# Attention values with their low halves stacked beside them in the mixer of a two-block transformer kernel

## The chip, the cores and the metric

The kernel runs as one program on one core of a Trainium2 chip. The metric is the device time of one execution in microseconds. Three runs of the kernel before gave a median of 1433.6 us, the lowest 1432.47, the highest 1434.11.

## The reference

The program computes two blocks on an input of 512 tokens by 1024 features, in float32. The first block has a mixer (a state-space branch and an attention branch side by side), a merge of the two and a feed-forward part; the second has two more mixers. The change sits in the attention branch of the first mixer, which has 8 heads of 64 features:

```python
def one_block(args):
    blk, q_blk = args
    q_pos = blk * Q_BLOCK + jnp.arange(Q_BLOCK)
    z = jnp.einsum('bqhd,bkhd->bhqk', q_blk, kf) * scale
    mask = key_pos[None, :] < q_pos[:, None]
    log_fail = jnp.where(mask, jax.nn.log_sigmoid(-z), 0.0)
    after = lax.cumsum(log_fail, axis=3, reverse=True) - log_fail
    log_w = jax.nn.log_sigmoid(z) + after
    w = jnp.where(mask, jnp.exp(log_w), 0.0)
    return jnp.einsum('bhqk,bkhd->bqhd', w, vf)
```

The last line is the product in question: for each head, the weights w (512 queries by 512 keys, below the diagonal) times the values of the head (512 keys by 64 features). The state-space branch, which shares the loop with it, is a recurrence per group of 16 channels, y = Re(C x) + D u with x_t = a x_(t-1) + b u_t, and runs in blocks of 4 tokens.

## The kernel before, in words

**Number format.** A float32 operand is kept as a rounded high half (fp32r) and a low half, the difference. A product of two such operands is three passes over TensorE into one PSUM bank: high times high, high times low, low times high. The helper `three` (L518 to L522) issues them; nearly all matrix products of the kernel go through it, and in the trace its lines L520, L521 and L522 are the three passes. `whi` and `wlo` are the split of a weight unit of 128 x 2048 elements: ScalarE writes `whi` (L1189), VectorE writes `wlo` (L1828).

**The mixer's loop.** The four iterations i = 0 to 3 are unrolled. Each handles four groups of the state-space branch (tiles ET, H, Es, X, M, U4) and two attention heads, hh = 0 and 1, whose features lie on partitions 0 to 63 and 64 to 127. The work of one iteration, on each engine, is written out by hand in program order, and semaphores tie the engines together. There is no planner: what is behind a waiting instruction on its engine waits too.

**Attention on each engine.** TensorE computes `scores(hh)`. ScalarE and VectorE make the logarithms of the failing probabilities in tile `att` (128 x 1280: four blocks of keys with 512, 384, 256 and 128 queries, packed), and split them into `athi` and `atlo`. TensorE adds their sums (`log_weights`, L725). ScalarE takes the exponential (L1345) and rounds it to `athi`, VectorE forms `atlo` (`w_lo`, L2114). Then `weigh_values(hh)` multiplies by the values: for each of four blocks of keys three passes with `vhi` or `vlo` as the stationary operand, 128 columns wide, that is the features of both heads, into PSUM bank 7. Of the 128 rows of the result only the 64 rows of head hh are wanted; ScalarE copies these to tile `ya` (`store`, L1352, in the trace L1189 with ya<-ps). `ya_done` counts these stores, and the next use of bank 7 waits for it.

**The values.** At the end of an iteration the values of the next two heads are transposed to bank 0; ScalarE rounds them to `vhi` (`values_hi`, L1270), VectorE writes `vlo` (`values_lo`, L2050).

**State-space steps that matter here.** VectorE makes the tables of the next iteration: `phase` (L2024 to L2030), which ends in `cosT`; ScalarE then forms the sine and the cosine (`table`, L1298 to L1303), with the loading of an activation table before and after. VectorE makes `ET` in `in_maps` (L1995 to L2002), and TensorE's `in_transposes` of the next iteration (L639) waits for it. In the middle of the iteration TensorE's `y` (L686) waits for VectorE's `X` (L2102). On VectorE the second half of an iteration is, in order: X, `fail_lo(1)`, `q_lo` of the next iteration, a weight split, `k_lo`, a weight split, `w_lo(1)`, `phase`, `ys` (L2137), `in_maps`, `values_lo`. On ScalarE it is `store(0)`, `k_evac`, a weight split, `y_tokens`, `weights(1)`, `evac_v`, `table`, `store(1)`, `evac_u`, `values_hi`. In the last iteration there are no `phase`, `table` and `in_maps`, and the merge follows.

**The same method elsewhere.** The attention of the second block (`fox`) holds its values in a tile `fvs` of 128 x 4 x 4 x 64, high and low halves side by side, uses two passes (L1042, L1044), and adds two halves of rows on VectorE (L2490).

Of the kernel before, what the change touches and what calls it, by code (L numbers as in the profile page):

```python
# [121 lines left out]
def build(nc, wstream, xT, pT, vecs_d, cst_d, s5p_d, wa2_d, outT):  # L122
    ctx = ExitStack()
    with ctx:
# [42 lines left out]
        with scope() as m:  # L167
            ys = sb("ys", [P, HC, T], F32, m)
            ya = sb("ya", [P, HC, T], F32, m)
            with scope() as e:  # L170
                blockpos = sb("blockpos", [P, NB], F32, e)
                s5p = sb("s5p", [P, 24, S5_PAIRS], F32, e)
                s5b = sb("s5b", [P, 4, 512], F32, e)
                uch = sb("uch", [P, L, NB], F32, e)
                vT = sb("vT", [P, T], F32, e)
                ET = sb("ET", [P, 2, QP, L, 32], F32, e)
                H = sb("H", [P, 2, QP, L + 1, 32], F32, e)
                decay = sb("decay", [P, QP, NB], F32, e)
                with scope() as s:
                    sq = sb("sq", [P, 2, T], F32, s)  # L180
                    un = sb("un", [P, 2, T], F32, s)
                    acc = sb("acc", [P, T], F32, s)
                    with scope() as pl:
                        pe_in = sb("pe_in", [P, 2, T], F32, pl)
                        pehi = sb("pehi", [P, 2, T], F32R, pl)
                        pelo = sb("pelo", [P, 2, T], F32R, pl)
                        pp = sb("pp", [P, DC, T], F32, pl)
                        sg = sb("sg", [P, 2, T], F32, pl)

                    sq2, acc2 = un, pp[:, 6, :]  # L190
                    cst_in = sb("cst_in", [P, 5, P], F32, s)
                with scope() as s:
                    qs = sb("qs", [P, 2, T], F32R, s)
                    kh = sb("kh", [P, 2, T], F32R, s)
                    atlo = sb("atlo", [P, NZ], F32R, s)
                    vhi = sb("vhi", [P, TT, P], F32R, s)
                    vlo = sb("vlo", [P, TT, P], F32R, s)
                    att = sb("att", [P, NZ], F32, s)
                    athi = sb("athi", [P, NZ], F32R, s)
                    Es = sb("Es", [P, 2, 512], F32, s)  # L200
                    kl = sb("kl", [P, 2, T], F32R, s)
                    tmp = sb("tmp", [P, QP, L + 1, 32], F32, s)
                    M = sb("M", [P, QP, P], F32, s)
                    cosT = sb("cosT", [P, QP, NB], F32, s)
                    sinT = sb("sinT", [P, QP, NB], F32, s)
                    rin = sb("rin", [P, 2, QP, NB], F32, s)
                    zst = sb("zst", [P, 2, QP, NB], F32, s)
                    X = sb("X", [P, 2, QP, NB], F32, s)
                    U4 = sb("U4", [P, QP, NB], F32, s)
                    tT = sb("tT", [P, QP, P], F32, s)  # L210
                    s5w = sb("s5w", [P, 5, 2, 2, S5_PAIRS], F32, s)
                    gl = Es
# [304 lines left out]
        def _(pe):  # L517
# [139 lines left out]
            def mixer(i, last=False):  # L657
# [70 lines left out]

                def weigh_values(hh):
                    if i or hh:  # L730
                        pe.wait_ge(ya_done, i * 2 + hh)
                    pe.wait_ge(w_ready, i * 2 + (hh + 1))
                    for kb in range(TT):
                        n = T - kb * P
                        three(ps[:, VB, kb * P:], vhi[:, kb, :], vlo[:, kb, :], athi[:, KB_AT[kb]:KB_AT[kb] + n],
                              atlo[:, KB_AT[kb]:KB_AT[kb] + n], kb == 0, kb == TT - 1,
                              pv_done if kb == TT - 1 else None)

                n = i * 2 + 2
                scores(0)  # L740
# [30 lines left out]

            def merge():
                n = U_MERGE
                pe.wait_ge(ya_done, 2 * HC)
                pe.wait_ge(ys_done, HC)
                pe.wait_ge(y_ready, HC)
                gemm(n + 2, (n + 2) % 2, [(m * P, 0, HC, 0, 4 + m) for m in range(4)], 512, yhi, ylo)
# [406 lines left out]
        def _(act):  # L1184
# [82 lines left out]

            def values_hi(i):
                act.wait_ge(v_tr, i + 1)
                copy(vhi[:, :, :], ps[:, 0, :].rearrange("p (t c) -> p t c", t=TT)).then_inc(v_hi, 1)  # L1270

            def evac_u(i, bank=1):
                act.wait_ge(block_done, i * 4 + 4)
# [113 lines left out]
            def merge():  # L1387
# [4 lines left out]
                own.sync()  # L1392
                for c in range(HC):
                    copy(yhi[:, c, :], ys[:, c, :]).then_inc(ye_hi, 1)
                act.wait_ge(ya_done, 2 * HC)
                for c in range(HC):
                    copy(ahi[:, c, :], ya[:, c, :]).then_inc(ye_hi, 1)

# [423 lines left out]
        def _(dve):  # L1822
# [224 lines left out]

            def values_lo(i):
                dve.wait_ge(v_hi, i + 1)
                V.tensor_tensor(vlo[:, :, :], ps[:, 0, :].rearrange("p (t c) -> p t c", t=TT), vhi[:, :, :],  # L2050
                                ALU.subtract).then_inc(v_ready, 1)

            def blocks(i):

# [3 lines left out]
            def mixer(i, last=False):  # L2058
# [53 lines left out]
                def w_lo(hh):  # L2112
                    dve.wait_ge(w_hi, i * 2 + (hh + 1))
                    V.tensor_tensor(atlo[:, :], att[:, :], athi[:, :], ALU.subtract).then_inc(w_ready, 1)  # L2114

                out_maps(i)
                softplus(0)
                fail_lo(0)
# [7 lines left out]
                if not last:  # L2126
                    q_lo(i + 1)
                split_lo(2 * i + 3, 1)
                if not last:
                    k_lo(i + 1)  # L2130
                split_lo(2 * i + 4, 0)
                w_lo(1)
                if not last:
# [2 lines left out]
                dve.wait_ge(y_tr, i + 1)  # L2136
                V.scalar_tensor_tensor(ys[:, i, :].rearrange("p (n b) -> p b n", b=L), uch[:, :, :], vec("D_skip", i),  # L2137
                                       ps[:, 6, :].rearrange("p (b n) -> p b n", b=L), ALU.mult, ALU.add).then_inc(ys_done, 1)
                if not last:
                    in_maps(i + 1)  # L2140
                    values_lo(i + 1)
# [630 lines left out]
```

## Time and profile before

| | |
|---|---|
| median of 3 runs | 1433.6 us (1432.47 to 1434.11) |
| the profiled execution | 1433.77 us, its span 1432.0 us |
| granted TensorE clock, mean over the span | 0.993 |
| TensorE busy | 1391.4 us, 97% of the span |
| VectorE busy | 963.1 us, 67% |
| ScalarE busy | 736.3 us, 51% |
| the mixer's loop | about 45 to 224 us of the span |

The span is the profiled stretch of one execution; its own time has 1.8 us around it. A matmul's end is modelled: consecutive matmuls overlap in the trace, so the distance between their starts, and not the duration of one, tells what TensorE takes for each. Engines run side by side, so a share of busy time alone doesn't say which of them another one waits for; the rows on waits do.

### The profile page before, as it was taken

The page shows a single profiled execution, that of the slowest core. Times are in us where ns is not written, and L with a number is a line of the kernel's source. Part 1 is how long each engine was busy: PE and PEld are TensorE (multiplying, and loading weights), DVE is VectorE, ACT ScalarE, POOL GpSimd, SP SyncE. Part 2 cuts the span into 40 slices and gives each one's busy share as a digit, 9 for nine tenths or more (in the row PEclk, how much of TensorE's full clock was granted, in tenths as well). Part 3 has the DMA queues.
Part 4 walks back from the last instruction along what each step waited for, and adds up shares of the span by engine and source line. Part 5 has one row for each costly group of instructions (what it writes and reads, how often), then busy time and mean ns, then how long its engine had stood idle before and what let it go on. Part 6 is the DMA issues. An engine that isn't in the chain of part 4 may idle for free.

```text
span 1432.0 us, 18411 instructions
## 1 busy us (share of the span) xinstructions
PE 1391.4 (97%) x6984; PEld 1165.1 (81%) x6984; DVE 963.1 (67%) x1343; ACT 736.3 (51%) x1038; POOL 70.3 (5%) x81
## 2 busy tenths in 40 slices
PE   7999999999999999999999999999999999999997
PEld 4888887888888888888877998878878888887876
DVE  7999885425544444444468867544879999998574
ACT  6767776232332222322255444333658888888452
POOL 2000000000200000000020000002100000000211
PEclk9999999999999999999999999999999999999998
DMA  6111102222322232223221211322221121211311
GB/s 215 49 59 59 60 1 107 94 94 88 118 68 109 88 118 88 88 88 112 94 89 59 89 59 59 104 88 89 88 89 59 61 86 59 87 60 42 120 60 59
DMA packets 19241, 118.22 MB, mean 83 GB/s; under 512 B 2400, under 2 KB 3680, under 8 KB 5616
## 3 DMA queue, kind: packets, MB, share of 16 engines
q1 hardware_dynamic: 18896, 116.38, 22.8%
q0 software_dynamic: 288, 1.05, 0.2%
q8 instruction: 40, 0.66, 0.2%
q14 instruction: 17, 0.14, 0.0%
HBM read 115.32 MB, written 2.10 MB: 82 GB/s over the span
## 4 chain that ended last, share of the span: by engine, by line
PE 75%; DVE 6%; ACT 2%; issue 1%; POOL 0%; DVEq 0%; ACTq 0%; POOLq 0%
PE ps L520 23%; PE ps L522 22%; PE ps L521 22%; PE ps L1011 1%; PE ps L1044 1%; PE ps L1001 1%; PE ps L1042 1%; DVE wlo L1828 1%; PE ps L1003 1%; DVE st L2310 1%; DVE stlo L2313 1%; ACT sthi L1189 1%; POOL pp L503 0%; ACT whi L1189 0%; PE ps L616 0%
## 5 line engine op out<-in xcount | busy, mean ns | idle before, releaser
L520 PE MATMUL ps<-uhi,whi 128*128 128x512 f32 x1100 | 436.7, 397 | 7.5 <-DVE ulo L2347 3.7
L522 PE MATMUL ps<-uhi,wlo 128*128 128x512 f32 x1100 | 430.4, 391 | 0.0
L521 PE MATMUL ps<-ulo,whi 128*128 128x512 f32 x1100 | 429.6, 391 | 0.0
L1828 DVE TENSOR_TENSOR wlo<-wraw,whi 128x2048 fp32r<-128x2048 f32 x104 | 241.0, 2320 | 99.6 <-ACT whi L1189 98.1
L1189 ACT ACTIVATE whi<-wraw 128x2048 fp32r<-128x2048 f32 x105 | 200.3, 1908 | 162.5 <-PE ps L522 160.5
L520 PEld LDWEIGHTS ps<-uhi,whi 128*128 128x128 f32 x1100 | 207.5, 189 | 54.7 <-issue 5.9
L522 PEld LDWEIGHTS ps<-uhi,wlo 128*128 128x128 f32 x1100 | 207.1, 188 | 44.6
L521 PEld LDWEIGHTS ps<-ulo,whi 128*128 128x128 f32 x1100 | 207.5, 189 | 40.4
L520 PE MATMUL ps<-hdhi,whi 128*128 128x512 f32 x256 | 99.6, 389 | 0.0
L521 PE MATMUL ps<-hdlo,whi 128*128 128x512 f32 x256 | 99.6, 389 | 0.0
L522 PE MATMUL ps<-hdhi,wlo 128*128 128x512 f32 x256 | 99.6, 389 | 0.0
L1467 ACT ACTIVATE hd<-rl 128x512 f32<-128x512 f32 x32 | 20.2, 632 | 116.9 <-DVE rl L2214 116.9
L2223 DVE TENSOR_TENSOR h<-ps,h 128x512 f32<-128x512 f32 x64 | 43.8, 690 | 44.1 <-PE ps L522 44.1
L2214 DVE SCALAR_TENSOR_TENSOR rl<-ps,rms_ff 128x512 f32<-128x512 f32 x32 | 22.0, 689 | 72.3 <-PE ps L522 70.3
L521 PEld LDWEIGHTS ps<-hdlo,whi 128*128 128x128 f32 x256 | 48.0, 188 | 10.1
L520 PEld LDWEIGHTS ps<-hdhi,whi 128*128 128x128 f32 x256 | 48.0, 188 | 10.0
L522 PEld LDWEIGHTS ps<-hdhi,wlo 128*128 128x128 f32 x256 | 48.0, 188 | 9.9
L1207 ACT ACTIVATE sq<-h 128x512 f32<-128x512 f32 x48 | 29.0, 621 | 39.0 <-DVE h L2193 19.8
L397 POOL TENSOR_TENSOR acc<-acc,sq 128x512 f32<-128x512 f32 x25 | 41.0, 1642 | 81.5 <-ACT sq L1207 80.3
L2193 DVE TENSOR_TENSOR h<-ps,h 128x512 f32<-128x512 f32 x24 | 16.5, 689 | 41.5 <-PE ps L522 41.4
L2219 DVE TENSOR_TENSOR hdlo<-hd,hdhi 128x512 fp32r<-128x512 f32 x32 | 20.7, 689 | 33.9 <-ACT hdhi L1189 33.9
L1658 ACT ACTIVATE pr<-ps,nmax 128x512 f32<-128x512 f32 (+1 forms) x64 | 32.8, 524 | 10.6 <-DVE nmax L2455 10.6
(444 smaller groups left out, 2475.6 us busy)
## 6 DMA issues: line engine op xcount, KB each, us to landing
wraw<-wstream SPq DMA_DIRECT2D x105, 1024.0 KB, 4.7
h<-xT SPq DMA_DIRECT2D x4, 512.0 KB, 5.5
outT<-h SPq DMA_DIRECT2D x8, 256.0 KB, 2.9
s5b<-s5p_d SPq DMA_DIRECT2D x1, 1024.0 KB, 12.1
pe_in<-pT POOLq DMA_DIRECT2D x2, 512.0 KB, 3.8
cst_in<-cst_d SPq DMA_DIRECT2D x5, 64.0 KB, 10.1
reset<-cst_d SPq DMA_DIRECT2D x1, 256.0 KB, 11.1
ones<-cst_d SPq DMA_DIRECT2D x1, 64.0 KB, 2.2
```

The source lines that it names most:

```text
L397: eng.tensor_tensor(acc[:, :], sq[:, 0, :] if c == 1 else acc[:, :], sq[:, c % 2, :], ALU.add).then_inc(acc_done, 1)
L520: nc.tensor.matmul(out, lh, rh, start=start, stop=False, skip_group_check=True)
L521: nc.tensor.matmul(out, lh, rl_, start=False, stop=False, skip_group_check=True)
L522: mm = nc.tensor.matmul(out, ll, rh, start=False, stop=stop, skip_group_check=True)
L1189: return A(out, in_, ACT.Copy, scale=scale)
L1207: A(sq[:, c % 2, :], h[:, c, :], ACT.Square).then_inc(sq_done, 1)
L1467: A(hd[:, m % 2, :], rl[:, m % 2, :], ACT.Square).then_inc(hd_done, 1)
L1658: e = A(pr[:, at], zf[:, at], ACT.Exp, bias=nmax[:, col], accum_out=rsum[:, col])
L1828: V.tensor_tensor(wlo[:, slot, :], wraw[:, slot, :], whi[:, slot, :], ALU.subtract).then_inc(lo_done, 1)
L2214: V.scalar_tensor_tensor(rl[:, m % 2, :], ps[:, a + m, :], 0.0, rms_ff[:, :], ALU.max, ALU.mult).then_inc(rl_done, 1)
L2219: V.tensor_tensor(hdlo[:, m, :], hd[:, m % 2, :], hdhi[:, m, :], ALU.subtract).then_inc(hd_ready, 1)
L2223: V.tensor_tensor(h[:, m, :], ps[:, bank, :], h[:, m, :], ALU.add).then_inc(h_added, 1)
```

## The change

Tiles `vhi` and `vlo` (each 128 x 4 x 128) become one tile `vs` (128 x 4 x 4 x 64). Within a block of keys its four parts of 64 columns are: head 0 high, head 0 low, head 1 low, head 1 high. For head hh the two parts 2 hh and 2 hh + 1 are one stationary operand of 128 columns. A pass with it gives the product with the head's high half in the 64 rows of the head, and the product with its low half in the other 64 rows. So a block of keys takes two passes, one with `athi` and one with `atlo`, and the product of the two low halves, which was left out before, is now computed too. ScalarE stores the head's rows to `ya` as before, and VectorE's new function `add_low_values(hh)` waits for that store, reads the other 64 rows of bank 7 and adds them to `ya`. `ya_done` now counts two steps a head, so that the next use of bank 7 and the merge wait for the addition.

```diff
@@ -193,8 +193,7 @@
                     qs = sb("qs", [P, 2, T], F32R, s)
                     kh = sb("kh", [P, 2, T], F32R, s)
                     atlo = sb("atlo", [P, NZ], F32R, s)
-                    vhi = sb("vhi", [P, TT, P], F32R, s)
-                    vlo = sb("vlo", [P, TT, P], F32R, s)
+                    vs = sb("vs", [P, TT, 4, 64], F32R, s)
                     att = sb("att", [P, NZ], F32, s)
                     athi = sb("athi", [P, NZ], F32R, s)
                     Es = sb("Es", [P, 2, 512], F32, s)
@@ -728,13 +727,16 @@
 
                 def weigh_values(hh):
                     if i or hh:
-                        pe.wait_ge(ya_done, i * 2 + hh)
+                        pe.wait_ge(ya_done, i * 4 + 2 * hh)
                     pe.wait_ge(w_ready, i * 2 + (hh + 1))
                     for kb in range(TT):
                         n = T - kb * P
-                        three(ps[:, VB, kb * P:], vhi[:, kb, :], vlo[:, kb, :], athi[:, KB_AT[kb]:KB_AT[kb] + n],
-                              atlo[:, KB_AT[kb]:KB_AT[kb] + n], kb == 0, kb == TT - 1,
-                              pv_done if kb == TT - 1 else None)
+                        stack = vs[:, kb, 2 * hh:2 * hh + 2, :].rearrange("p s c -> p (s c)")
+                        for part in (athi, atlo):
+                            mm = nc.tensor.matmul(ps[:, VB, kb * P:], stack, part[:, KB_AT[kb]:KB_AT[kb] + n],
+                                                  start=kb == 0 and part is athi, stop=kb == TT - 1 and part is atlo,
+                                                  skip_group_check=True)
+                    mm.then_inc(pv_done, 1)
 
                 n = i * 2 + 2
                 scores(0)
@@ -771,7 +773,7 @@
 
             def merge():
                 n = U_MERGE
-                pe.wait_ge(ya_done, 2 * HC)
+                pe.wait_ge(ya_done, 4 * HC)
                 pe.wait_ge(ys_done, HC)
                 pe.wait_ge(y_ready, HC)
                 gemm(n + 2, (n + 2) % 2, [(m * P, 0, HC, 0, 4 + m) for m in range(4)], 512, yhi, ylo)
@@ -1267,7 +1269,7 @@
 
             def values_hi(i):
                 act.wait_ge(v_tr, i + 1)
-                copy(vhi[:, :, :], ps[:, 0, :].rearrange("p (t c) -> p t c", t=TT)).then_inc(v_hi, 1)
+                copy(vs[:, :, 0:4:3, :], ps[:, 0, :].rearrange("p (t h c) -> p t h c", t=TT, h=2)).then_inc(v_hi, 1)
 
             def evac_u(i, bank=1):
                 act.wait_ge(block_done, i * 4 + 4)
@@ -1392,7 +1394,7 @@
                 own.sync()
                 for c in range(HC):
                     copy(yhi[:, c, :], ys[:, c, :]).then_inc(ye_hi, 1)
-                act.wait_ge(ya_done, 2 * HC)
+                act.wait_ge(ya_done, 4 * HC)
                 for c in range(HC):
                     copy(ahi[:, c, :], ya[:, c, :]).then_inc(ye_hi, 1)
 
@@ -2047,8 +2049,8 @@
 
             def values_lo(i):
                 dve.wait_ge(v_hi, i + 1)
-                V.tensor_tensor(vlo[:, :, :], ps[:, 0, :].rearrange("p (t c) -> p t c", t=TT), vhi[:, :, :],
-                                ALU.subtract).then_inc(v_ready, 1)
+                V.tensor_tensor(vs[:, :, 1:3, :], ps[:, 0, :].rearrange("p (t h c) -> p t h c", t=TT, h=2),
+                                vs[:, :, 0:4:3, :], ALU.subtract).then_inc(v_ready, 1)
 
             def blocks(i):
 
@@ -2113,6 +2115,12 @@
                     dve.wait_ge(w_hi, i * 2 + (hh + 1))
                     V.tensor_tensor(atlo[:, :], att[:, :], athi[:, :], ALU.subtract).then_inc(w_ready, 1)
 
+                def add_low_values(hh):
+
+                    dve.wait_ge(ya_done, i * 4 + 2 * hh + 1)
+                    rows = HEAD_ROWS[hh]
+                    V.tensor_tensor(ya[rows, i, :], ps[HEAD_ROWS[1 - hh], 7, :], ya[rows, i, :], ALU.add).then_inc(ya_done, 1)
+
                 out_maps(i)
                 softplus(0)
                 fail_lo(0)
@@ -2126,6 +2134,7 @@
                 if not last:
                     q_lo(i + 1)
                 split_lo(2 * i + 3, 1)
+                add_low_values(0)
                 if not last:
                     k_lo(i + 1)
                 split_lo(2 * i + 4, 0)
@@ -2136,6 +2145,7 @@
                 dve.wait_ge(y_tr, i + 1)
                 V.scalar_tensor_tensor(ys[:, i, :].rearrange("p (n b) -> p b n", b=L), uch[:, :, :], vec("D_skip", i),
                                        ps[:, 6, :].rearrange("p (b n) -> p b n", b=L), ALU.mult, ALU.add).then_inc(ys_done, 1)
+                add_low_values(1)
                 if not last:
                     in_maps(i + 1)
                     values_lo(i + 1)
```

What follows are pieces of the order in which the instructions stand. On TensorE, the first `weigh_values`, which is the same piece for every head; in the kernel before:

```order
L520 MATMUL ps<-athi,vhi 128x512 [waits att_w_ready]
L521 MATMUL ps<-atlo,vhi 128x512
L522 MATMUL ps<-athi,vlo 128x512
L520 MATMUL ps<-athi,vhi 128x384
L521 MATMUL ps<-atlo,vhi 128x384
L522 MATMUL ps<-athi,vlo 128x384
L520 MATMUL ps<-athi,vhi 128x256
L521 MATMUL ps<-atlo,vhi 128x256
L522 MATMUL ps<-athi,vlo 128x256
L520 MATMUL ps<-athi,vhi 128x128
L521 MATMUL ps<-atlo,vhi 128x128
L522 MATMUL ps<-athi,vlo 128x128
```

and in the changed kernel:

```order
L736 MATMUL ps<-athi,vs 128x512 [waits att_w_ready]
L736 MATMUL ps<-atlo,vs 128x512
L736 MATMUL ps<-athi,vs 128x384
L736 MATMUL ps<-atlo,vs 128x384
L736 MATMUL ps<-athi,vs 128x256
L736 MATMUL ps<-atlo,vs 128x256
L736 MATMUL ps<-athi,vs 128x128
L736 MATMUL ps<-atlo,vs 128x128
```

Four matmuls of twelve are gone; nothing else moves on TensorE.

On VectorE, the second half of an iteration (0 to 2) from `q_lo` of the next iteration to `w_lo(1)`, in the changed kernel; the kernel before has the same rows without the one of `ya`, two lines lower in number:

```order
L2041 SCALAR_TENSOR_TENSOR qs<-ps,qs 64x512 [waits qk_hi] x2
L1830 TENSOR_TENSOR wlo<-wraw,whi 128x2048 [waits weights_hi_done]
L2122 TENSOR_TENSOR ya<-ps,ya 64x512 [waits att_stored]
L2048 TENSOR_TENSOR kl<-ps,kh 64x512 [waits qk_hi] x2
L1830 TENSOR_TENSOR wlo<-wraw,whi 128x2048 [waits weights_hi_done]
L2116 TENSOR_TENSOR atlo<-att,athi 128x1280 [waits att_w_hi]
```

The addition for head 0 stands between the two weight splits, and waits for the store of head 0.

On VectorE, the end of `phase` and the start of `in_maps`, in the kernel before:

```order
L2028 TENSOR_TENSOR rin<-rin 128x512 [waits dve_own_steps]
L2029 TENSOR_SCALAR rin<-rin 128x512 [waits dve_own_steps]
L2030 TENSOR_TENSOR cosT<-rin 128x512 [waits dve_own_steps]
L2137 SCALAR_TENSOR_TENSOR ys<-uch,vecs,ps 128x4x128 [waits s5_y_transposed]
L1995 TENSOR_TENSOR ET<-s5b,s5w 128x512 [waits s5_in_maps_transposed]
L1996 TENSOR_TENSOR tmp<-s5b,s5w 128x4x128
```

and in the changed kernel, with the addition for head 1 between `ys` and `in_maps`:

```order
L2030 TENSOR_TENSOR rin<-rin 128x512 [waits dve_own_steps]
L2031 TENSOR_SCALAR rin<-rin 128x512 [waits dve_own_steps]
L2032 TENSOR_TENSOR cosT<-rin 128x512 [waits dve_own_steps]
L2146 SCALAR_TENSOR_TENSOR ys<-uch,vecs,ps 128x4x128 [waits s5_y_transposed]
L2122 TENSOR_TENSOR ya<-ps,ya 64x512 [waits att_stored]
L1997 TENSOR_TENSOR ET<-s5b,s5w 128x512 [waits s5_in_maps_transposed]
L1998 TENSOR_TENSOR tmp<-s5b,s5w 128x4x128
```

The store that this addition waits for stands on ScalarE behind the whole of `table`, in the changed kernel as in the one before:

```order
L1191 ACTIVATE vT<-ps 128x512 [waits block_done]
L1300 ACT_TABLE_LOAD
L1300 ACTIVATE sinT<-cosT 128x512 [waits s5_phase]
L1302 ACTIVATE cosT<-cosT 128x512 [waits act_own_steps]
L1304 ACTIVATE cosT<-cosT,biases 128x512 [waits act_own_steps]
L1305 ACT_TABLE_LOAD
L1191 ACTIVATE ya<-ps 64x512 [waits att_out]
L1191 ACTIVATE uch<-ps 128x512 [waits s5_chunk,block_done]
```

ScalarE's order is unchanged: `table` waits for VectorE's `cosT`, and `ya` comes after it.

## Rows read from the trace of the kernel before

**Rows 1.** The page: busy time of the engines (share of the span), instructions.

```profile
PE 1391.4 (97%) x6984; PEld 1165.1 (81%) x6984; DVE 963.1 (67%) x1343; ACT 736.3 (51%) x1038; POOL 70.3 (5%) x81
```

**Rows 2.** Waits of TensorE: who waited, for whom, us in total, times, longest.

```profile
PE ps L725 <- DVE atlo L2110: 3.7, 4, 1.7
...
PE ps L686 <- DVE X L2102: 2.7, 4, 0.7
...
PE ps L639 <- DVE ET L2002: 1.4, 3, 0.5
```

**Rows 3.** Timeline of VectorE, iteration 1: start, us, engine, line, operation.

```profile
117.50 0.69 DVE L2102 TENSOR_TENSOR X<-X,rin 128x508 f32<-128x508 f32 x1
...
123.49 1.41 DVE L2046 TENSOR_TENSOR kl<-ps,kh 64x512 fp32r<-64x512 f32 x2
...
127.14 1.49 DVE L2114 TENSOR_TENSOR atlo<-att,athi 128x1280 fp32r<-128x1280 f32 x1
...
132.36 0.69 DVE L2030 TENSOR_TENSOR cosT<-rin 128x512 f32<-128x512 f32 x1
133.09 1.16 DVE L2137 SCALAR_TENSOR_TENSOR ys<-uch,vecs,ps 128x512 f32<-128x512 f32 x1
134.08 0.68 DVE L1995 TENSOR_TENSOR ET<-s5b,s5w 128x512 f32<-128x512 f32 x1
```

**Rows 4.** Timeline of ScalarE, iteration 1; in brackets the idle time before.

```profile
118.20 0.59 ACT L1189 ACTIVATE ya<-ps 64x512 f32<-64x512 f32 x1
...
125.29 1.28 ACT L1189 ACTIVATE athi<-att 128x1280 fp32r<-128x1280 f32 x1
...
133.09 0.63 ACT L1298 ACTIVATE sinT<-cosT 128x512 f32<-128x512 f32 x1 [1.65 <-DVE cosT L2030]
...
135.16 1.28 ACT L1303 ACT_TABLE_LOAD   x1
136.45 0.59 ACT L1189 ACTIVATE ya<-ps 64x512 f32<-64x512 f32 x1
...
141.43 1.24 ACT L1331 ACTIVATE att<-ps 128x1280 f32<-128x1280 f32 x1 [0.60 <-PE ps L712]
```

**Rows 5.** Timeline of TensorE, iteration 1: head 1's values, then the iteration's end.

```profile
129.34 0.39 PE L520 MATMUL ps<-athi,vhi 128*128 128x512 f32 x1
...
131.19 0.62 PE L696 MATMUL ps<-ident,tT 128*128 128x128 f32 x4
...
137.12 0.60 PE L628 MATMUL ps<-ident,vT 128*128 128x128 f32 x4
138.19 1.09 PE L639 MATMUL ps<-ident,ET 128*128 128x128 f32 x8 [0.48 <-DVE ET L2002]
```

**Rows 6.** Tiles vlo and fvs, VectorE: duration ns min/median/max, first and last start.

```profile
L2050 DVE TENSOR_TENSOR vlo<-ps,vhi x4: 690/692/692, 46.9 to 184.7; 128x512 fp32r<-128x512 f32 x4
```
```profile
L2447 DVE TENSOR_TENSOR fvs<-ps,fvs x8: 671/692/693, 1085.2 to 1309.1; 128x512 fp32r<-128x512 f32 x8
```

**Rows 7.** Timeline of VectorE, last iteration and merge.

```profile
219.07 1.50 DVE L2114 TENSOR_TENSOR atlo<-att,athi 128x1280 fp32r<-128x1280 f32 x1 [2.48 <-ACT athi L1189]
224.33 1.12 DVE L2137 SCALAR_TENSOR_TENSOR ys<-uch,vecs,ps 128x512 f32<-128x512 f32 x1 [3.77 <-PE ps L696]
228.66 2.50 DVE L2148 TENSOR_TENSOR ylo<-ys,yhi 128x512 fp32r<-128x512 f32 x4 [3.21 <-ACT yhi L1189]
```

**Rows 8.** Windows of 2 us: busy (instructions) of each engine; granted clock; DMA.

```profile
1304.00:1306.00 2.00, 0.43 (x3) 0.32 (x3) 1.97 (x4) 1.95 (x4) 0.00 (x0) 1.00 0.48 98
1306.00:1308.00 2.00, 2.00 (x6) 1.53 (x6) 2.00 (x6) 1.18 (x5) 0.00 (x0) 0.57 1.01 426
1308.00:1310.00 2.00, 2.00 (x7) 1.56 (x6) 1.58 (x6) 2.00 (x9) 0.00 (x0) 0.58 0.00 0
```

**Rows 9.** Timeline of TensorE, first 22 us.

```profile
7.25 5.46 PE L585 MATMUL ps<-M 128*128 128x512 f32 x6 [7.25 <-DMA h<-xT]
...
18.42 2.74 PE L585 MATMUL ps<-M 128*128 128x512 f32 x6
```

## The prediction

> **What bounds the kernel now.** I read the page first: TensorE is busy 97% of the span, VectorE 67% [rows 1]. By that alone a pass less on TensorE is time saved. But matmul durations overlap in the trace, so 97% hides waits, and the mixer has to be read by itself. The table of waits says where TensorE stands still there: three places in an iteration, and each time for VectorE [rows 2]. It waits in `log_weights` for `atlo` (3.7 us in 4 iterations), in `y` for `X` (2.7 us in 4, 0.7 each) and in `in_transposes` for `ET` (1.4 us in 3, 0.5 each). So TensorE arrives early at all three, and VectorE sets the pace. Next the timeline of VectorE from `X` to `ET` [rows 3]: none of these rows has idle time in brackets. From 117.50 us, where X is finished, to `in_maps` at 134.08 us and on to ET, VectorE goes from one instruction to the next without a wait. Even `w_lo(1)`, which needs ScalarE's `athi`, starts at 127.14 us when athi has been ready since 125.29 + 1.28 = 126.57 us [rows 4]. Whatever is added to VectorE between X and ET makes the iteration longer. The last view is ScalarE's timeline of the same stretch [rows 4]: it waits 1.65 us for `cosT`, works through the sine table until 136.44 us and only then stores head 1 to `ya`, at 136.45 us. In the kernel before nobody needs that store soon. TensorE finished head 1's product at about 131.19 us [rows 5].
>
> **The pass that goes.** A head's product takes from 129.34 to 131.19 us, 1.85 us for 12 matmuls [rows 5]; four of them, one of each width, are a third, 0.62 us. Over 8 heads this is 4.9 us of TensorE, and that would be the gain if TensorE set the pace. In iterations 0 to 2 it doesn't: head 0's 0.62 us lies ahead of `y`, which waits 0.7 us for X already and would wait 1.3; head 1's lies ahead of `in_transposes`, which waits 0.5 us for ET. What is saved turns into a longer wait: 0. In iteration 3, head 0's saving meets the wait for X again. Head 1's counts: there VectorE's `ys` waits 3.77 us for TensorE's transposes (L696), which stand right behind the product [rows 7], and the merge follows from ys and the store. I take -0.6 us for the whole kernel.
>
> **The values' new layout.** The same number of elements is written in runs of 64. The second block's tile `fvs` has this layout, and VectorE's low half takes 692 ns there as `vlo` does here [rows 6]. 0. For ScalarE's copy, whose pattern changes in the same way, I take 0 as well: TensorE reads the values only in the product, long after, and VectorE will reach `values_lo` 4.4 us later (below), so even a copy twice as slow would be hidden.
>
> **The addition for head 0.** It reads PSUM and SBUF, 64 x 512. The nearest instruction is `kl<-ps,kh` of the same shape, two in 1.41 us, 0.70 us each [rows 3]. Its store ended at 118.20 + 0.59 = 118.79 us [rows 4], VectorE arrives at about 123.49, so it waits for nothing. It costs its 0.7 us in full, since w_lo(1) has no slack behind it: cosT is ready 0.7 us later, and so is all of ScalarE's `table`. In iteration 3 w_lo(1) waits 2.48 us for ScalarE [rows 7], which hides it: 0.
>
> **The addition for head 1.** This is the large term. It stands between ys and in_maps and waits for store(1), which stands on ScalarE behind the table. That table waits for the cosT of the same VectorE: VectorE hands over cosT and then waits until ScalarE has gone through a sine, an absolute value, a second sine and the loading of an activation table. In numbers of iteration 1: the store ended at 136.45 + 0.59 = 137.04 us; with the 0.7 us of head 0's addition, 137.75. The addition takes 0.7 us, in_maps starts at 138.5 instead of 134.08 us [rows 3, 4]: 4.4 us, of which 0.7 is head 0's addition, 3.0 a wait and 0.7 the addition itself. Queued behind the waiting instruction are in_maps, values_lo and the next iteration's out_maps. TensorE's `in_transposes` waits for in_maps, and behind it stand the next `scores`, for which ScalarE already waits 0.60 us [rows 4]. So nothing in the next iteration can catch up: all three engines start it 4.4 us later. Bounds: if ScalarE's store came at once, 1.4 us an iteration; if the addition were as slow as the 1.16 us of ys [rows 3], 5.3. I take 4.4. Three iterations: +13.2 us. In iteration 3 there is no in_maps; the next VectorE instruction, ylo, waited 3.21 us for ScalarE, whose work follows the store anyway [rows 7], and that hides the addition.
>
> **The clock.** TensorE now has a hole at each of the three ends: 0.5 us as before, 4.4 us more, and 0.6 us by which it comes earlier, 5.5 us from the end of the transposes at 137.7 us [rows 5]. What a hole does is seen in this trace: at 1304 to 1306 us TensorE was busy for 0.43 us of 2, and in the 4 us behind it the granted clock is 0.57 and 0.58 (the lower level, 1.2 GHz, for most of it) [rows 8]. That is 4 x 0.425 = 1.7 us lost. At the program's start, after 7.25 us of nothing, six long matmuls took 5.46 us where six of the same took 2.74 us later, 2.7 us lost [rows 9]. Behind my holes stands just what the chain needs from TensorE: the transposes and the scores, for which ScalarE waits. A slower clock there is paid in full. Bounds 0 and 2.7 us a hole; I take the 1.7 of the hole that lies in mid-program, as mine do: +5.1 us.
>
> The Trainium skill ("TensorE: Matmul & The Clock Gate", section "HAM oscillation — how this bites in real kernels") has the rule that pauses between bursts of matmuls, if long enough, put the clock back to half, so that every burst starts slow. By that rule all three holes would cost a slow stretch, 1451.5 us; without it the sum would be 1446.4 us. The trace agrees as far as it goes [rows 8].
>
> **The sum,** against the profiled execution's own 1433.77 us, which is 0.2 us above the median of the runs: 1433.8 - 0.6 + 13.2 + 5.1 = 1451.5 us; with the 0.2 us off for the median and rounded, 1451 us.
>
> **Rivals.**
> A. The wait comes, the clock stays at 2.4 GHz: 1433.8 - 0.6 + 13.2 = 1446.4 us. For it: waits of TensorE of 1 to 2 us elsewhere, in the mixer too, mostly cost nothing. Against: mine are 5.5 us, and a shorter pause sufficed at 1304 us. Chance 0.13.
> B. The clock stays low longer, as at the program's start: 3 x 2.7 us, 1454.5 us, and with a slow addition (0.5 us more in each of three) 1456. For it: a 5.5 us hole is nearer to the 7.25 us of the start. Against: the start had no work before it. Chance 0.09.
> C. VectorE loses only the two additions: store(1) gets in before the table, or the wait is covered. Then 3 x 1.4 - 0.6: 1437.4 us. Against: ScalarE takes its work in order. Chance 0.03.
> D. The other side: TensorE sets the pace and the kernel is faster. The mechanism is the passes removed, 8 x 0.62 us, with the additions hidden in VectorE's gaps: 1433.8 - 4.9 = 1428.9 us. It decides from the point where store(1) is finished before VectorE gets to it and VectorE has 1.4 us to spare between X and ET. For it stands TensorE's 97% [rows 1]; against it that VectorE has no idle time there and TensorE has [rows 2, 3]. Chance 0.03.
>
> **How the numbers follow.** The forecast (the wait, and a clock that falls at two or three of the holes) has 0.72. Its own range is 1449 to 1453.5 us. The range reaches from A with a little less (1445) to B (1456). A difference under 0.2%, 2.9 us, can't be told from none here. Faster by more is D, 0.03; within it nothing but parts of C and D, 0.01; slower by more is the rest, 0.96.
>
> **What would show it.** In the changed kernel's profile: VectorE idle before the second ya addition in three iterations, about 3.0 us each, put down to ScalarE's ya; in_maps 4.4 us later against cosT's old place (3.7 us against its new one); TensorE idle before `in_transposes` for about 5.5 us in each of three; the granted clock under 1 in the windows behind these holes; iterations 0 to 2 longer by 4.4 us plus the clock's share; iteration 3 and everything from the merge on as before. Additions of 0.7 us, eight matmuls a head in 1.2 us. I would be wrong if the second addition had no wait, if in_transposes came without a hole, or if the iterations were longer and no VectorE wait stood in them. If only the clock's term is off, the granted clock is 1.00 behind the holes (A) or the low stretches are longer than 4 us (B).

## The result: 1.35% slower, 1451 us predicted and 1452.7 measured

The changed kernel took 1452.66 us (median of 4 runs, 1451.56 to 1454.26), the kernel before in the same comparison 1433.31 us: ratio 1.0135, 95% interval 1.0119 to 1.0150. The profiled execution took 1451.84 us with a span of 1450.1 us, 18.1 us longer than the span before. The two medians are 19.35 us apart; what follows explains the 18.1 us of the two profiled executions, and the rest is not traced to a place.

The page of the changed kernel has nearly the same busy times as [rows 1]; the share of TensorE fell because the span grew:

```profile
PE 1391.4 (96%) x6952; PEld 1166.2 (80%) x6952; DVE 967.7 (67%) x1351; ACT 735.9 (51%) x1038; POOL 70.8 (5%) x81
```

32 matmuls are gone, 8 additions have come, and 18 us are in neither. TensorE's busy time didn't even fall by what the 32 matmuls had taken, because others ran longer, as the clock further down shows; in a kernel with as few passes whose clock stayed up in the mixer (the one without the third pass, below) it is 1385.1 us. The 18 us are in the waits. First TensorE's, as in [rows 2]:

```profile
PE ps L638 <- DVE ET L2004: 16.0, 3, 5.3
...
PE ps L685 <- DVE X L2104: 5.2, 4, 1.3
PE ps L724 <- DVE atlo L2112: 3.7, 4, 1.7
```

The wait for ET went from 1.4 to 16.0 us in three iterations; the one for X from 0.7 to 1.3 us each, which is head 0's saving turned into a wait. Then what the other engines waited for between 40 and 245 us:

```profile
DVE ya L2122 <- ACT ya L1191: 8.6, 3, 2.9
...
DVE U L2058 <- PE ps L653: 6.3, 3, 2.7
ACT att L1333 <- PE ps L711: 5.5, 4, 2.3
```

The first row is the new wait of VectorE's addition for ScalarE's store. The other two stand behind a slow TensorE: VectorE did not wait for `u_blocks` (the row of tile U) at all before, and ScalarE's 0.60 us for the scores [rows 4] became up to 2.3. VectorE's timeline in iteration 1, beside [rows 3]:

```profile
122.53 0.69 DVE L2104 TENSOR_TENSOR X<-X,rin 128x508 f32<-128x508 f32 x1
...
128.41 0.68 DVE L2122 TENSOR_TENSOR ya<-ps,ya 64x512 f32<-64x512 f32 x1
...
138.00 0.69 DVE L2032 TENSOR_TENSOR cosT<-rin 128x512 f32<-128x512 f32 x1
138.72 1.15 DVE L2146 SCALAR_TENSOR_TENSOR ys<-uch,vecs,ps 128x512 f32<-128x512 f32 x1
142.71 0.68 DVE L2122 TENSOR_TENSOR ya<-ps,ya 64x512 f32<-64x512 f32 x1 [2.85 <-ACT ya L1191]
143.43 0.69 DVE L1997 TENSOR_TENSOR ET<-s5b,s5w 128x512 f32<-128x512 f32 x1
```

and ScalarE's, beside [rows 4]:

```profile
138.72 0.63 ACT L1300 ACTIVATE sinT<-cosT 128x512 f32<-128x512 f32 x1 [2.27 <-DVE cosT L2032]
...
140.79 1.28 ACT L1305 ACT_TABLE_LOAD   x1
142.09 0.59 ACT L1191 ACTIVATE ya<-ps 64x512 f32<-64x512 f32 x1
```

The chain reads: cosT at 138.69 us, the sine table on ScalarE until 142.07, the store until 142.68, the addition at 142.71, in_maps at 143.43. From X to in_maps it is 20.9 us where it was 16.58: 4.3 us more. TensorE sees this as a pause:

```profile
134.41 0.47 PE L736 MATMUL ps<-athi,vs 128*128 128x512 f32 x1
...
135.71 0.62 PE L695 MATMUL ps<-ident,tT 128*128 128x128 f32 x4
...
141.63 0.60 PE L627 MATMUL ps<-ident,vT 128*128 128x128 f32 x4
147.56 1.97 PE L638 MATMUL ps<-ident,ET 128*128 128x128 f32 x8 [5.33 <-DVE ET L2004]
```

Eight matmuls of a head take 1.30 us in place of 1.85 [rows 5], and the eight transposes behind the pause take 1.97 us in place of 1.09. Windows of 4 us around the holes; the last three columns are the granted clock, the DMA share and GB/s:

```profile
92.00:96.00 4.00, 0.91 (x5) 0.91 (x6) 3.90 (x7) 0.00 (x0) 0.00 (x0) 0.54 0.00 0
96.00:100.00 4.00, 4.00 (x21) 3.81 (x21) 2.66 (x4) 1.51 (x2) 0.00 (x0) 0.61 0.00 0
...
148.00:152.00 4.00, 4.00 (x25) 3.91 (x24) 3.13 (x5) 1.51 (x2) 0.00 (x0) 0.71 0.00 0
...
200.00:204.00 4.00, 4.00 (x18) 3.81 (x17) 3.02 (x4) 1.51 (x2) 0.00 (x0) 0.50 0.00 0
```

Behind each of the three holes TensorE ran at 1.2 GHz for a while (a granted clock of 0.50 is that level; the other values are windows in which it changed). An iteration is best measured from X to X. Before, X started at 71.25, 117.50 [rows 3] and

```profile
163.74 0.69 DVE L2102 TENSOR_TENSOR X<-X,rin 128x508 f32<-128x508 f32 x1
...
209.98 0.69 DVE L2102 TENSOR_TENSOR X<-X,rin 128x508 f32<-128x508 f32 x1
```

46.24 us each time (46.25 the first). Now it starts at 70.07, 122.53 and

```profile
174.42 0.69 DVE L2104 TENSOR_TENSOR X<-X,rin 128x508 f32<-128x508 f32 x1
...
227.57 0.69 DVE L2104 TENSOR_TENSOR X<-X,rin 128x508 f32<-128x508 f32 x1
```

52.46, 51.89 and 53.15 us, together 18.8 us more. From X to ET it is 4.3 us more in each (13.0); from ET to the next X 1.9, 1.3 and 2.6 us more (5.8), and that part has no added work in it. The last iteration and the merge are 0.6 us shorter (18.04 us from X to ylo, 18.68 before). The first X comes 1.2 us earlier than before, and the rest of the program behind ylo takes 1.1 us more (1204.5 us, 1203.3 before). The edit adds or removes no instruction behind ylo, and such differences stand between kernels that do the same there: the first X came 0.9 us earlier with the wait alone, too. The two nearly cancel, so the sum of the parts in between, 18.2 us, is close to the 18.1 us of the spans.

### The profile page after: what moved, and what is told of

Same layout as the page of the kernel before. It is cut to its first block, busy times and chain, and to the rows that moved or that the text cites. A ratio compares the mean times of both kernels' runs of the same rounds, so it can differ in the third digit from the quotient of the medians.

```text
span 1450.1 us, 18355 instructions
## 1 busy us (share of the span) xinstructions
PE 1391.4 (96%) x6952; PEld 1166.2 (80%) x6952; DVE 967.7 (67%) x1351; ACT 735.9 (51%) x1038; POOL 70.8 (5%) x81
## 4 chain that ended last, share of the span: by engine, by line
PE 73%; DVE 7%; ACT 3%; issue 1%; POOL 0%; DVEq 0%; ACTq 0%; POOLq 0%
PE ps L519 22%; PE ps L521 22%; PE ps L520 22%; PE ps L1013 1%; DVE wlo L1830 1%; PE ps L1046 1%; PE ps L1003 1%; PE ps L1044 1%; PE ps L1005 1%; DVE st L2320 1%; DVE stlo L2323 1%; ACT sthi L1191 1%; ACT whi L1191 1%; POOL pp L502 0%; DVE un L1898 0%
```

## The experiments

**Is the wait enough by itself?** The kernel before, with only the wait:

```diff
+                dve.wait_ge(ya_done, i * 2 + 2)
                 if not last:
                     in_maps(i + 1)
```

> The kernel before, three passes and no addition, with one wait added: VectorE waits for the store of head 1 ahead of in_maps. My theory: the store ends at 137.04 us where in_maps started at 134.08, so 3.0 us an iteration, 9.0 us, and a clock that falls behind TensorE's pauses of 3.5 us, 4 to 5 us more: 1446 to 1448 us. If the clock stays: 1442.3 us. Rival (the wait is hidden elsewhere): 1433 us.

Measured: 1446.79 us (1445.26 to 1447.98), ratio 1.0089, interval 1.0072 to 1.0105. VectorE's timeline has the wait, and its X rows (the first of the pair) give the iterations:

```profile
121.43 0.68 DVE L2100 TENSOR_TENSOR X<-X,rin 128x508 f32<-128x508 f32 x1
...
141.73 0.69 DVE L1995 TENSOR_TENSOR ET<-s5b,s5w 128x512 f32<-128x512 f32 x1 [2.84 <-ACT ya L1189]
...
172.17 0.68 DVE L2100 TENSOR_TENSOR X<-X,rin 128x508 f32<-128x508 f32 x1
...
221.45 0.68 DVE L2100 TENSOR_TENSOR X<-X,rin 128x508 f32<-128x508 f32 x1
```

and TensorE's, with the pause ahead of `in_transposes` in brackets:

```profile
94.06 1.97 PE L639 MATMUL ps<-ident,ET 128*128 128x128 f32 x8 [3.49 <-DVE ET L2002]
...
145.87 1.10 PE L639 MATMUL ps<-ident,ET 128*128 128x128 f32 x8 [3.49 <-DVE ET L2002]
...
196.60 1.10 PE L639 MATMUL ps<-ident,ET 128*128 128x128 f32 x8 [3.49 <-DVE ET L2002]
```

With X at 69.63 us ahead of these, the iterations are 51.80, 50.74 and 49.28 us: 5.6, 4.5 and 3.0 us longer. The third is the wait alone; behind TensorE's third pause of 3.5 us the granted clock stayed at 1.00. The first two had a fall behind the same pause (0.58 and 0.57 from 92 to 100 us, 0.90 and 0.67 from 144 to 152 us), 2.5 and 1.5 us more. So a wait with no addition and no new layout makes two thirds of the loss (12.8 of 19.4 us).

**Does the wait go when the store is early?** The changed kernel with ScalarE's order turned:

```diff
                     evac_v(i + 1)
-                    table(i + 1)
                 store(1)
                 if not last:
+                    table(i + 1)
                     evac_u(i + 1)
```

> The changed kernel, with ScalarE's store of head 1 moved ahead of the sine table, so that VectorE's second addition finds it done. My theory: the 3.0 us wait of VectorE in each of three iterations goes, the two additions (0.7 us each) stay, so 1433.3 + 3 x 1.4 - 0.6 = 1437 us; TensorE's pause before the transposes shrinks from 5.3 us to about 2.5 us and the clock mostly stays up (up to 1.7 us a pause more, 1442, if it doesn't). Rival: the additions or the new layout themselves are what costs, and the store is not: about 1452 us, as the changed kernel.

Measured: 1439.99 us (1437.72 to 1441.18), ratio 1.0041, interval 1.0026 to 1.0055: 12.7 us below the changed kernel, and 3 us above what I expected. The addition has no wait now:

```profile
137.35 0.69 DVE L2122 TENSOR_TENSOR ya<-ps,ya 64x512 f32<-64x512 f32 x1
138.07 0.69 DVE L1997 TENSOR_TENSOR ET<-s5b,s5w 128x512 f32<-128x512 f32 x1
```

Its iterations are 49.35, 47.78 and 47.76 us. The two additions cost 1.5 us an iteration where I took 1.4, and the first iteration had a fall of the clock behind a pause of 2.5 us, 1.6 us more; behind the same pause in the other two the clock stayed at 1.00. This is the trace of the fastest of the five executions, 1437.72 us, which is near what I expected. The slower three took 1440 to 1441 us at a mean granted clock of 0.991 to 0.992, where the profiled one had 0.995; more falls of the clock would make that difference, but no trace of those executions shows them. The rival, at 1452 us, is out.

**And if nothing waits for the addition?** ScalarE as in the changed kernel, VectorE's addition for head 1 behind in_maps:

```diff
+                if not last:
+                    in_maps(i + 1)
                 add_low_values(1)
                 if not last:
-                    in_maps(i + 1)
                     values_lo(i + 1)
```

> The changed kernel, with VectorE's second addition moved behind in_maps (ahead of values_lo); ScalarE's order as it is. My theory: nothing of the chain waits for this addition any more, only head 0's addition lengthens VectorE's path: 1433.3 + 3 x 0.7 - 0.6 = 1434.8 us. Rival (VectorE's busy time as such is the bound in the mixer): both additions count, 1437 us. Rival (the store's place on ScalarE costs in another way): above 1440 us.

Measured: 1435.04 us (1433.9 to 1435.82), ratio 1.0007, interval 0.9997 to 1.0017. The same work in another place, 17.6 us less, as expected, and not to be told from the kernel before. The addition has no wait here:

```profile
137.81 0.69 DVE L2004 TENSOR_TENSOR ET<-ET,tmp 128x512 f32<-128x512 f32 x1
138.54 0.68 DVE L2122 TENSOR_TENSOR ya<-ps,ya 64x512 f32<-64x512 f32 x1
```

**What does the clock cost?** The changed kernel with 20 matmuls that nobody reads in TensorE's pause:

```diff
                     transpose_values(i + 1)
+                    pe.wait_ge(w_exp, i * 2 + 2)
+                    for _ in range(20):
+                        nc.tensor.matmul(ps[:, 2, :], uhi[:, 0, 0:P], ulo[:, 0, :], start=True, stop=True)
                     in_transposes(i + 1)
```

> The changed kernel, with 20 matmuls of 128x512 whose result nobody reads issued on TensorE behind the transposes of the values, some 4.6 us in the pause before in_transposes. My theory: the wait for ET stays as long, but the clock doesn't fall behind it; the iterations lose the 1.3 to 2.6 us each from ET to X (5.8 us in the three by the two traces): 1452.7 - 5.8 = 1446.9 us. Rival (the stretch from ET to X is longer for another reason, such as what stands behind VectorE's late values_lo): no change, 1452.7 us.

Measured: 1445.17 us (1445.12 to 1447.24), ratio 1.0083, interval 1.0066 to 1.0100. TensorE's timeline and the windows:

```profile
140.31 4.83 PE L772 MATMUL ps<-ulo,uhi 128*128 128x512 f32 x20
145.90 1.09 PE L638 MATMUL ps<-ident,ET 128*128 128x128 f32 x8 [0.76 <-DVE ET L2007]
```
```profile
144.00:148.00 4.00, 3.25 (x22) 2.62 (x21) 3.96 (x7) 0.97 (x2) 0.00 (x0) 1.00 0.00 0
148.00:152.00 4.00, 4.00 (x25) 3.55 (x25) 3.72 (x5) 3.34 (x5) 0.00 (x0) 1.00 0.01 4
```

The transposes are back at 1.09 us and the clock at 1.00. The iterations are 50.56, 50.59 and 50.60 us: 4.34 us above the kernel before each time, the wait and the additions, and nothing else. VectorE still waits 2.85 us for the store; its wait for `u_blocks` went from 6.3 to 0.3 us and ScalarE's for the scores from 5.5 to 2.4, so those two came from the clock. Against the changed kernel the three iterations are 5.75 us shorter, which is the clock's part. The medians differ by 7.5 us and the two profiled executions by 6.7; of that last difference 1.2 us lie behind ylo, where the edit changes nothing.

**What is the pass worth?** First the kernel before without the third pass; the product with the values' low half is left out:

```diff
-                        three(ps[:, VB, kb * P:], vhi[:, kb, :], vlo[:, kb, :], ...
+                        for part in (athi, atlo):
+                            mm = nc.tensor.matmul(ps[:, VB, kb * P:], vhi[:, kb, :], part[...], ...
...
+                    mm.then_inc(pv_done, 1)
```

> The kernel before without the third pass of weigh_values (the product with the values' low half is left out, and nothing is added on VectorE): the saving by itself. My theory: VectorE sets the pace, so only head 1 of the last iteration counts: 0.6 us less, 1433.3 us against 1433.9, with the pauses ahead of y and of in_transposes 0.6 us longer. Rival (TensorE sets the pace): 8 x 0.62 us less, 1429.0 us.

Measured: 1432.18 us (1431.58 to 1433.05), ratio 0.9992, interval 0.9983 to 1.0001. The iterations stay at 46.23 us, and the time saved stands in the waits, beside [rows 2]:

```profile
PE ps L686 <- DVE X L2104: 5.2, 4, 1.3
...
PE ps L639 <- DVE ET L2004: 3.3, 3, 1.1
```

0.6 us more at each of the places where TensorE waits for VectorE. The merge's ylo comes 0.7 us earlier, near the 0.6 expected; the median is 1.5 us below the 1433.65 us of the kernel before in this comparison, and the interval includes no change. The rival's 1429 us (0.9967) is outside the interval. Next, kernels with room on VectorE. `phase` of iterations 1 to 3 goes to GpSimd:

```diff
+            for i in range(1, HC):
+                pool.wait_ge(x_ready, i)
...
+                step(G(a, pos, turns[0], ALU.mult))
+                step(nc.gpsimd.tensor_scalar(b, a, ROUND, ROUND, ALU.add, ALU.subtract))
...
+                G(cosT[:, :, :], a, b, ALU.subtract).then_inc(phase_ready, 1)
```

> The kernel before, with `phase` of iterations 1 to 3 on GpSimd instead of VectorE (seven operations of 128x512, about 1.6 us each, from X on) and in_maps ahead of ys. VectorE has 4.9 us an iteration less between X and ET, so TensorE doesn't wait for ET any more (0.5 us in each of three). My theory: 1.5 us less, 1432.4 us. Rival (GpSimd and VectorE slow each other): more than 1434 us.

> The changed kernel with `phase` of iterations 1 to 3 on GpSimd, in_maps ahead of ys, and ScalarE's store of head 1 ahead of the sine table. Now VectorE has room between X and ET, so TensorE sets the pace there and head 1's shorter product counts in every iteration: 0.5 + 0.6 us in each of three and 0.6 in the last, 2.4 to 3.9 us less than the kernel before, 1430 to 1431.5 us, and below pool_three by 0.6 us x 4. Rival (the pass saved is worth nothing even with room on VectorE): equal to pool_three or above.

Measured: with three passes 1434.94 us (ratio 1.0011, interval 1.0002 to 1.0020), with two 1434.07 us (1.0002, interval 0.9992 to 1.0011). Neither gained what I expected. The timelines of the three-pass kernel show why; GpSimd, then VectorE's `w_lo(1)`, then TensorE:

```profile
125.58 3.21 POOL L507 TENSOR_TENSOR rin<-rin 128x512 f32<-128x512 f32 x1
```
```profile
127.57 2.57 DVE L2127 TENSOR_TENSOR atlo<-att,athi 128x1280 fp32r<-128x1280 f32 x1
```
```profile
130.28 0.47 PE L533 MATMUL ps<-athi,vhi 128*128 128x512 f32 x1 [1.02 <-DVE atlo L2127]
```

While both engines ran, w_lo(1) took 2.57 us in place of 1.49 [rows 3] and GpSimd's operations up to 3.2 us. TensorE then waited for the weights. The rival on GpSimd was right. But the pair bears on the question: with TensorE held up ahead of the product, an iteration is 46.83 us with three passes and 46.19 with two, 0.64 us less. So a pass seems worth its 0.62 us where nothing waits behind it. The medians are only 0.9 us apart, where four times 0.6 was forecast, and the two-pass kernel differs in more than the pass: it has the two additions and the early store, which weren't taken apart.

Last, five of the seven operations of phase moved, on VectorE itself, to where it waits for ScalarE:

```diff
                 out_maps(i)
+                if not last:
...
+                    phase_part(i + 1, (0,))
                 softplus(0)
+                if not last:
+                    phase_part(i + 1, (1, 2))
                 fail_lo(0)
                 turn_in()
+                if not last:
+                    phase_part(i + 1, (3, 4))
                 w_lo(0)
...
-                    phase(i + 1)
+                    phase_part(i + 1, (5, 6))
```

> The kernel before (three passes) with five of the seven operations of the next iteration's phase moved, on VectorE itself, into the places of the same iteration where VectorE waits for ScalarE (0.9, 1.3 and 1.7 us ahead of softplus(0), fail_lo(0) and w_lo(0)); the last two stay where they were. My theory: VectorE gets 3.4 us of room between X and ET, TensorE sets the pace there, its wait for ET (0.5 us in each of three) goes: 1.5 us less than the kernel before, 1432.2 us. Rival (the moved operations don't fit the waits and lengthen the stretch from ET to X): 1434 us or more.

> The changed kernel (two passes, both additions on VectorE) with the same move of phase, and ScalarE's store of head 1 ahead of the sine table. With room on VectorE the additions are hidden and head 1's shorter product counts in all four iterations. My theory: 0.5 + 0.6 us in each of three iterations and 0.6 us in the last, 3.9 us less than the kernel before: 1429.8 us, 2.4 us below gap_three. Rival (a pass saved is worth nothing): equal to gap_three, 1432 us.

Measured: 1434.22 us with three passes (ratio 1.0004, interval 0.9995 to 1.0013), 1432.69 with two (0.9995, interval 0.9986 to 1.0004). Both missed by 2 to 3 us; with three passes the rival has the better number. There are two causes. First, the moved operations don't all fit. In the three-pass kernel TensorE no longer waits for ET, but ahead of `log_weights` it waits for `atlo`:

```profile
151.40 0.50 PE L725 MATMUL ps<-athi,trir 128*128 128x512 f32 x1 [1.29 <-DVE atlo L2129]
```

That wait was 0.67 us in the kernel before, so the 0.5 us gained in one place are lost in the other. The iterations are 46.18, 46.19 and 45.57 us, against 46.24: the first two gained nothing, and only the third, which ends in the last iteration, where no operation was put ahead, is shorter. In the two-pass kernel they are 45.67, 45.63 and 45.40 us, 0.6 to 0.8 us less than before, where 1.1 was forecast. Second, the first X came late, at 72.69 us with two passes and 72.99 with three, where it was 71.25. In the first iteration VectorE had no wait ahead of softplus(0). TensorE's pause ahead of `log_weights` was 2.6 us there in place of 1.7, and the granted clock fell behind it; with two passes:

```profile
72.69 0.69 DVE L2123 TENSOR_TENSOR X<-X,rin 128x508 f32<-128x508 f32 x1
```
```profile
56.00:58.00 2.00, 0.62 (x3) 0.53 (x4) 2.00 (x2) 1.53 (x1) 0.00 (x0) 1.00 0.00 0
58.00:60.00 2.00, 2.00 (x12) 2.00 (x11) 2.00 (x3) 0.00 (x0) 0.00 (x0) 0.66 0.00 0
60.00:62.00 2.00, 2.00 (x11) 2.00 (x11) 1.97 (x4) 0.24 (x1) 0.00 (x0) 0.50 0.04 8
```

Most of the delay is this fall: `log_weights` started 0.1 us later than before (57.38 us, 57.28 before), and the exponential behind it 1.4 us later (61.76 us, 60.32 before). So the first iteration got nothing ahead of softplus(0) (the five operations became three, in the two later waits):

> As gap_two, but in the first iteration nothing is put ahead of softplus(0), where VectorE has no wait, and only three operations into the two later waits; four stay behind w_lo(1). My theory: the first X comes 1.7 us earlier than in gap_two (72.7 us there, 71.3 before) and no slow stretch of the clock lies ahead of it, the iterations keep 45.6 us against 46.2: 1431 us, 2.5 us less than the kernel before. Rival (the time lost in gap_two was not in the first iteration): 1432.7 us as gap_two.

> As gap_three, with the first iteration arranged in the same way. My theory: 1.7 us less than gap_three and 1.5 to 2 us above gap_two_b, which is what head 1's pass is worth in four iterations: 1432.7 us. Rival (the pass is worth nothing): equal to gap_two_b.

Measured: two passes 1431.91 us (1430.71 to 1432.54), ratio 0.9988, interval 0.9979 to 0.9997; three passes 1432.55 us, ratio 0.9994, interval 0.9985 to 1.0003. X of the two-pass kernel starts at 71.24 us and

```profile
117.22 0.69 DVE L2123 TENSOR_TENSOR X<-X,rin 128x508 f32<-128x508 f32 x1
...
162.87 0.69 DVE L2123 TENSOR_TENSOR X<-X,rin 128x508 f32<-128x508 f32 x1
...
208.25 0.69 DVE L2123 TENSOR_TENSOR X<-X,rin 128x508 f32<-128x508 f32 x1
```

45.98, 45.65 and 45.38 us. TensorE's pause ahead of the first `log_weights` is 1.9 us now, and the clock stays at 1.00 behind it. This is the version that beats both kernels, by 1.8 us against the one before, 0.1% with an interval that ends below 1. It does the two passes and both additions. The expectation for the three-pass kernel, 1.5 to 2 us above it, missed: the medians are 0.6 us apart and their intervals overlap. That the two passes have a part in it is seen in the traces (X to X over three iterations 137.0 us, 138.0 with three passes), and in all three pairs the kernel with two passes has the lower median, by 0.9, 1.5 and 0.6 us. These pairs too differ in the additions and in the place of the store. The store's place is unlikely to be the cause here: in iteration 1 of both kernels ScalarE has done the store and the table and waits for TensorE before it goes on (0.65 us with two passes, 1.94 with three).

## Why the prediction was right

- **VectorE sets the pace, so the pass saves nothing in iterations 0 to 2.** Shown: without the pass the iterations stay at 46.23 us and both waits grow by 0.6 us. In the last iteration and the merge 0.6 us were gained, as said. A head's eight matmuls take 1.30 us, not the 1.2 of the prediction, so by the starts a pass is 0.55 us.
- **Head 0's addition, 0.7 us.** Nearly. It waits for nothing and costs 0.6 us in the iterations: in the kernel with the second addition behind in_maps the iterations are 46.83 to 46.87 us.
- **Head 1's addition waits for the store behind the sine table, 3.0 us.** Shown three ways: the row says 2.85 us; the wait alone costs 3.0 us; an earlier store removes it. The row is shorter than the cost by what the next instruction otherwise overlaps with ys. In the changed kernel the step from X to in_maps is 0.6 (head 0's addition), 3.0 (the wait) and 0.7 us (the addition itself), 4.3 us where I took 4.4. Only where there is no wait does the second addition cost 0.9 us (the early store: 1.5 us for both, less 0.6).
- **The clock.** I took 1.7 us a hole from a hole elsewhere; it was 1.9, 1.3 and 2.6 us, 5.8 in all against 5.1. That the clock is the cause is shown by the filled pause, which took the 5.8 us away with VectorE's wait unchanged and came out near rival A's 1446.4 us. That the size came out within 0.7 us is in part luck: one hole elsewhere gave the 1.7 us, with a pause of 1.6 us ahead of it and not 5.3, and the price of a fall varied from 1.3 to 2.6 us. Rival B, 2.7 us a hole, was nearly reached by one of three.
- **The sum.** The terms forecast were -0.6, +13.2 and +5.1 us, 17.7 in all; measured in the traces they were -0.6, +13.0 and +5.8, 18.2 in all. The medians differ by 19.35 us. What is missing of it lies in no term of the prediction.
- **The layout costs nothing.** VectorE's low half takes 681 ns (692 before [rows 6]), ScalarE's copy 592 ns, as before.
- **Rivals C and D** named conditions that experiments then made. With an early store (C) the fastest execution took 1437.7 us and the median 1440.0, where C said 1437.4: it had left out that the clock can fall behind the 2.5 us pause that remains. D needed room on VectorE; given that, two passes were faster than the kernel before, by 1.8 us and not by D's 4.9: head 0's saving still turned into a wait for X (1.3 us in each of the four iterations), and the first iteration had less room.

The 0.3 us by which the two additions differ, where nothing waits, can be read from the distances between starts. The instruction behind either addition starts 0.72 us after it. Head 0's saves 0.11 us in front: it starts 2.21 us after the weight split (125.86 after 123.65 us with the early store), where `kl` had started 2.32 us after it (123.49 after 121.17 us in the kernel before). Head 1's loses 0.19 us: with the early store it starts 1.18 us after ys, which runs 1.15 us, where in_maps had started 0.99 us after it [rows 3]. The Trainium skill ("VectorE: DVE Perf Modes", section "Two Vector instructions with no wait between them") says that an instruction starts only when everything earlier has finished if what it reads from a memory starts in another group of 32 partitions than what the last reader of that memory read, or what it writes starts in another group than the last output there. The addition for head 1 reads and writes `ya` from row 64 on, behind an instruction whose rows start at 0: the trace agrees, 1.18 us against the 1.15 that ys runs. It was not tested by itself.

## What to carry to other kernels

Work taken from a busy engine is worth only as much as the next wait of that engine leaves: subtract the wait that it will meet before counting a gain. When a step is added that waits for another engine's by-product, look at where that by-product stands in the other engine's order, because a copy that nobody needed soon may be queued behind a long job, and behind one that waits for the very engine that now waits. A pause made on TensorE can be paid a second time through its clock, in the work that the chain needs first. The cheapest cure here was to move the new step behind the work that others wait for: 17.6 us of the loss went when one call changed its place.

## What the runs showed of the hardware

- Pauses of TensorE in the mixer and what the granted clock did behind them: 5.3 us (the changed kernel), a fall each of three times; 3.5 us (the wait alone), two of three; 2.5 us (the early store), one of three; 2.6 us ahead of the first `log_weights` (five operations of phase moved), two of two; 1.9 us in the same place (the later pair), none of two; 1.6 us (the addition behind in_maps), none of three. But in the kernel before, a pause of 1.57 us up to 1305.75 us has a fall behind it [rows 8]. The length of the pause alone doesn't settle it. Ahead of `in_transposes` a fall cost 1.3 to 2.6 us, and the same pause of 3.5 us in the same kernel cost 0, 1.5 or 2.5 us.
- GpSimd and VectorE, each on SBUF operands alone, got in each other's way, but not always: beside GpSimd a 128x1280 subtraction on VectorE took 2.57 us in place of 1.49, one 128x2048 subtraction 2.95 us and another its usual 2.29. GpSimd's seven operations of 128x512 took between 1.04 and 3.21 us; what they take with VectorE at rest was not measured.
- An addition of 64x512 with one PSUM operand takes 0.68 us and costs between 0.6 and 0.9 us of the engine, by what stands ahead of and behind it.
